# Squares of the keys in a prompt's attention summed from two rounded parts, one or two turns later

## The reference, cut to what matters

```python
def rmsnorm(x, g):
    xf = x.astype(jnp.float32)
    y = xf * lax.rsqrt(jnp.mean(xf * xf, axis=-1, keepdims=True) + EPS)
    return (y * g.astype(jnp.float32)).astype(x.dtype)

def mla_prompt(q_nope, q_rope, c_kv, k_rope, w_uk, w_uv, g_kn):
    k_nope = rmsnorm(jnp.einsum('btc,chd->bthd', c_kv, w_uk), g_kn)
    v = jnp.einsum('btc,chd->bthd', c_kv, w_uv)
    ...
        s = jnp.einsum('bqhd,bkhd->bhqk', qn, k_nope) + jnp.einsum('bqhr,bkr->bhqk', qr, k_rope)
        p = jax.nn.softmax(jnp.where(mask, s.astype(jnp.float32) * SOFTMAX_SCALE, -jnp.inf), axis=-1)
        return jnp.einsum('bhqk,bkhd->bqhd', p.astype(v.dtype), v)
```

## Time and the profile before

| | us |
|---|---|
| median of 3 runs | 1902.29 |
| lowest and highest | 1901.44, 1902.49 |
| the profiled execution | 1903.54 |
| its span in the trace | 1901.7 |
| TensorE busy in it | 1872.1 (98%) |
| VectorE, ScalarE, GpSimd busy | 1098.8, 904.0, 806.1 |

### The profile page before, as it was taken

The page is one execution under the profiler, slowest core; times in us unless marked ns, Lnnn a source line. Parts: engine busy times, 40 slices in busy tenths (PEclk is TensorE's granted clock), DMA queues, the critical chain, the costliest instruction groups (busy, mean ns, idle before and its releaser), DMA issues.

```text
span 1901.7 us, 35322 instructions
## 1 busy us (share of the span) xinstructions
PE 1872.1 (98%) x13021; PEld 1802.9 (95%) x13021; DVE 1098.8 (58%) x1950; ACT 904.0 (48%) x1858; POOL 806.1 (42%) x814
## 2 busy tenths in 40 slices
PE   7999999999999999999999999999999999999998
PEld 7886679999999999999999999999999999999998
DVE  4677756565556555544645644547773564564464
ACT  4456655554555455343424333347754342433333
POOL 3340013432223224253473474385755347347435
PEclk9999999999999999999999999999999999999999
DMA  5320101211111110222333232232222233323223
GB/s 153 67 57 3 26 20 44 80 33 47 35 39 32 48 35 17 71 80 78 89 89 88 78 98 81 79 109 78 75 79 78 78 88 90 88 83 95 77 86 97
DMA packets 253093, 131.63 MB, mean 69 GB/s; under 512 B 43073, under 2 KB 250754, under 8 KB 252882
## 3 DMA queue, kind: packets, MB, share of 16 engines
q1 hardware_dynamic: 252514, 128.56, 24.2%
q10 hardware_dynamic: 444, 1.29, 0.2%
HBM read 126.21 MB, written 3.61 MB: 68 GB/s over the span
## 4 chain that ended last, share of the span: by engine, by line
PE 94%; DVE 3%; ACT 1%; issue 1%; DMA 1%; SPq 0%; POOL 0%; DVEq 0%; ACTq 0%; POOLq 0%
PE ps L208 13%; PE ps L211 13%; PE ps L209 13%; PE ps L1275 7%; PE ps L1273 7%; PE ps L1274 7%; PE ps L1912 5%; PE ps L1910 5%; PE ps L1916 5%; PE ps L1303 3%; PE ps L259 2%; PE ps L251 2%; PE ps L252 2%; PE ps L1049 2%; PE ps L1240 2%; PE ps L265 1%
## 5 line engine op out<-in xcount | busy, mean ns | idle before, releaser
L208 PE MATMUL ps<-split,whi 128*128 128x288 f32 x1840 | 541.6, 296 | 1.4 <-DVE arena L807 1.0
L209 PE MATMUL ps<-split,whi 128*128 128x288 f32 x1840 | 539.0, 294 | 0.0
L211 PE MATMUL ps<-split,wlo 128*128 128x288 f32 x1840 | 526.7, 295 | 0.0
L195 POOL TENSOR_TENSOR wlo<-raw,whi 128x1024 fp32r<-128x1024 f32 x127 | 307.4, 2423 | 377.7 <-ACT whi L172 370.3
L208 PEld LDWEIGHTS ps<-split,whi 128*128 128x128 f32 x1840 | 345.3, 188 | 3.7 <-issue 3.0
L209 PEld LDWEIGHTS ps<-split,whi 128*128 128x128 f32 x1840 | 345.2, 188 | 0.4
L211 PEld LDWEIGHTS ps<-split,wlo 128*128 128x128 f32 x1840 | 339.9, 188 | 0.0
L1273 PE MATMUL ps<-split,split 128*128 128x384 f32 x768 | 268.2, 349 | 0.0
L1523 DVE TENSOR_REDUCE ssq<-arena 128x16 f32<-128x1024 f32 x128 | 156.1, 1220 | 186.6 <-ACT arena L1385 186.6
L1385 ACT ACTIVATE arena<-ps 128x384 f32<-128x384 f32 (+1 forms) x384 | 174.7, 457 | 184.4 <-PE ps L1275 181.4
L1275 PE MATMUL ps<-split,split 128*128 128x384 f32 x768 | 257.9, 336 | 0.0
(11 more groups left out here) (343 smaller groups left out, 3587.3 us busy)
## 6 DMA issues: line engine op xcount, KB each, us to landing
raw<-in_ffn_w_up SPq DMA_DIRECT2D x96, 512.0 KB, 3.7
raw<-in_ffn_w_down SPq DMA_DIRECT2D x48, 512.0 KB, 3.9
arena<-in_cache_ckv SPq DMA_DIRECT2D x128, 128.0 KB, 2.0
raw<-in_rec_w_in SPq DMA_DIRECT2D x16, 512.0 KB, 3.9
raw<-in_attn_w_o SPq DMA_DIRECT2D x8, 512.0 KB, 5.3
raw<-in_rec_w_out SPq DMA_DIRECT2D x8, 512.0 KB, 4.3
raw<-in_attn_w_down SPq DMA_DIRECT2D x7, 512.0 KB, 7.4
raw<-in_attn_w_uq SPq DMA_DIRECT2D x48, 64.0 KB, 2.1
```

What stands on the lines that cost most here:

```text
L195: pool.tensor_tensor(wlo[:, t % RING, :], raw[:, t % RING, :], f32(whi[:, t % RING, :]), ALU.subtract).then_inc(w_lo, 1)
L208: pe.matmul(o, wh, a, start=first, stop=False, skip_group_check=resumed)
L209: pe.matmul(o, wh, b, start=False, stop=False, skip_group_check=resumed)
L211: mm = pe.matmul(o, wl, a, start=False, stop=last, skip_group_check=resumed)
```

## The change

The sum of squares for pairs 1 to 7 is no longer a float32 product. ScalarE rounds the squares to float32r (`ksq_hi`), GpSimd subtracts that from the squares (`ksq_lo`, written over `sq[0]`), and TensorE multiplies both with a float32r copy of the ones (`blk64_hi`, made once on ScalarE), in four products. `key_sum` and `key_root` stand in unit 5 where they stood in unit 4, and `key_norm` in unit 6 where it stood in unit 4 (unit 5 for pair 1). The buffer `work` is allocated ahead of `smallg`.

```diff
+        k_hi, K_HI0 = u_ss, 12
+        k_lo, K_LO0 = u_rs, 12
+        ksq_hi = area(A_P + 7424, T, dt=F32R)
+        ksq_lo = nc.alloc_sbuf_tensor_at("ksq_lo", [P, T], F32R, offset=work_at)[:]
+        blk64_hi = area(A_P + 8000, P, dt=F32R)
+
         def key_sum(pe, j):
-            pe.wait_ge(k_sq, j + 1)
-            ones_product(pe, 4, blk64, sq[0]).then_inc(k_ss, 1)
+            if j == 0:
+                pe.wait_ge(k_sq, 1)
+                ones_product(pe, 4, blk64, sq[0]).then_inc(k_ss, 1)
+                return
+            pe.wait_ge(k_lo, K_LO0 + j)
+            for i, h, l in zip(range(2), halves(ksq_hi), halves(ksq_lo)):
+                pe.matmul(ps[:, 4 + i, 0:HT], blk64_hi, h, start=True, stop=False)
+                mm = pe.matmul(ps[:, 4 + i, 0:HT], blk64_hi, l, start=False, stop=True)
+            mm.then_inc(k_ss, 1)
+
+        def key_low(pool, j):
+            pool.wait_ge(k_hi, K_HI0 + j)
+            pool.tensor_tensor(ksq_lo, sq[0], f32(ksq_hi), ALU.subtract).then_inc(k_lo, 1)
+            pool.wait_ge(k_lo, K_LO0 + j)
...
         def key_square(act, j):
             act.wait_ge(k_ev, j + 1)
             act.activation(sq[0], kflat[j], ACT.Square).then_inc(k_sq, 1)
+            if j:
+                if j == 1:
+                    act.copy(blk64_hi, blk64)
+                act.wait_ge(k_sq, j + 1)
+                act.copy(ksq_hi, sq[0]).then_inc(k_hi, 1)
...
-                    if u % 8 == 4 and h // 2 < 7:
+                    if u % 8 == 5 and h // 2 < 7:
                         key_sum(pe, h // 2 + 1)
...
-                if u < UNITS and u % 8 == 4 and u // 8 < 7:
+                if u < UNITS and u % 8 == 5 and u // 8 < 7:
                     key_root(act, u // 8 + 1)
...
-                    if (u == 5 or u % 8 == 4 and u > 4) and h // 2 < 7:
+                    if u % 8 == 6 and h // 2 < 7:
                         key_norm(dve, h // 2 + 1)
...
+            for j in range(1, 8):
+                key_low(pool, j)
             sample_pool(pool)
```

More of the change, by code:

```diff
@@ L95, in build @@
         rpar = sb("rpar", [P, DC, R_ALL])
+        work_at = nc.sbuf_base
+        work = sb("work", [P, 5 * T])
         smallg = sb("smallg", [P, 12])
-        work = sb("work", [P, 5 * T])
         snew = sb("snew", [P, NB, HQ])
```

## The result

The changed kernel takes 1924.9 us, the median of 4 executions (1921.1 to 1931.4), against 1902.4 before: the ratio is 1.012, with a 95% interval from 1.0107 to 1.0133, some 22 us slower. The prediction had 1913.2 with a range up to 1917. Sign and place were right; the size forecast, 10.9 us, was half of what came. The profiled execution of one experiment, e11, was slow (2026.9 us at a mean clock of 0.851) and is left out of every ratio.

A forecast was written before the change was run, and what follows sets the result against it. TensorE was taken to bound the stage, closely, in a relay with VectorE and ScalarE. Five pairs (8.2 us), one (1.9) and pair 1 (0.8) gave 10.9 us, from 1902.3 to 1913.2 us, range 1907.5 to 1917.

The forecast's parts named there:

- The term that decides, root and placing without cover: Behind unit 5's scores: next head's scores wait for placed keys, starting 5.20 us later instead of 3.66; 1.54 us per covered pair.
- The hole where the sum stood: Behind unit 4's scores: the turn waits for ScalarE's copy behind the rounding; the 1.08 us saved is lost, 0.1 added.
- The sum of the waits: Over pairs 1 to 7: five at 1.64 us, one at 1.9, pair 1 at 0.8, together 10.9 us slower.
- The exponentials behind the copy slip by 0.7, but `attend` covers them: On ScalarE behind the turned row's copy: exponentials come 0.7 us later, hidden under the products of `attend`.
- GpSimd's subtraction: Between rounding and new sum: takes 1.43 us, has 2.3 us of slack, costs nothing.
- The rival that GpSimd and VectorE hold each other up: In pair 1, subtraction beside VectorE's scaling of unit 3's row: 0.5 to 1.5 us added, 1914 to 1915; 10 in 100.
- TensorE's saving as a gain of 3.8 us if nothing waited: Cheaper sum products on TensorE, 0.54 us a pair over seven pairs; as the faster rival 1898.5 us, 6 in 100.

The follow-up runs named there:

- e11: Kernel before with squares summed as float32r high part alone and, in the six covered pairs, the root ahead of unit 4's exponential: 1899.5 us (0.9982).
- e10: Changed kernel with an extra float32 product where the old sum stood, and the root of pairs 1 to 7 without its logarithm: 1916.8 us (1.0073).
- e1: Changed kernel with one unneeded float32 product of the old sum's shape where the old sum stood, in seven pairs: 1915.2 us (1.0065).
- e9: Changed kernel with an unneeded float32 product only ahead of each pair's first scores, the wait ahead of the turn left idle: 1923.9 us (1.011).
- e4: Changed kernel with ScalarE's rounding moved behind the copy of the turned row: 1913.3 us (1.0056).
- e7: Kernel before with only the rounding added on ScalarE behind the square, its result unused: 1908.1 us (1.0026).
- e8: Kernel before with squares of pairs 1 to 7 rounded and summed in float32r alone, low part left out, old places: 1902.6 us (0.9998).
- e2: Kernel before with only the move of sum, root and placing to units 5, 5 and 6, sum still float32: 1914.1 us (1.0058).
- e3: Changed kernel with sum, root and placing back in their old places: 1925.5 us (1.012).

## Why the prediction was wrong, point by point

- *The term that decides, root and placing without cover:* right. Keys 5.27 us behind unit 5's scores against 5.20; the wait of 1.03 us; the maximum of unit 7 at the placing's end (182.52 against the placing's 180.96 + 1.64). One sentence was too sharp: the chain is closed by ScalarE's root with only 0.15 us to spare against VectorE's own order (e10).
- *The hole where the sum stood:* right in place, short in size. "The turn can start at 198.27, that is 0.1 later than with the float32 sum": it is 0.28 later from the pair's first scores (190.22 - 182.75 = 7.47 against 198.17 - 190.98 = 7.19), since the square comes 0.08 later in its pair (5.47 us behind the first scores, 188.22 - 182.75, against 5.39, 196.37 - 190.98) and the turn follows the copy's end by 0.14 us, not by 0.04.
- *The sum of the waits:* 10.9 forecast, 12.6 measured with the clock held (e1). Five pairs at about 1.91 instead of 1.64, the pair with the extra work on VectorE 2.07 instead of 1.9, pair 1 1.01 instead of 0.8 (with the clock low behind its wait of 1.24 us it lost 2.06 in the changed kernel).
- *The step that failed* is that both waits were priced by their length alone. The prediction laid rows taken at full clock one behind the other ("at full granted clock") and never asked whether the clock would stay there with TensorE idle for 1.3 us in one piece. It did not: 1.7 us in each of six `attend`, 1.1 us in pair 1, and 9.7 us in the median of the changed kernel against that of e1. e1 shows the cause by taking only the idle away, e9 that in pairs 2 to 7 it is the wait ahead of the turn, e4 that with 0.7 us less of it `attend` runs at full clock. The Trainium skill, page "TensorE: Matmul & The Clock Gate", section "What's actually happening", says that the clock is set "based on how busy the PE has been recently" and knows the same two levels; the traces agree (0.57 over the 4.0 us behind the wait, 1.00 with it filled). The trace of the kernel before had a warning of its own, on none of the rows: TensorE stands idle for 3.57 us up to 18.15 us, and works at the lower level behind that.

```profile
14.60:18.10 3.50, 0.00 (x0) 0.00 (x0) 1.96 (x5) 2.90 (x5) 2.31 (x4) 0.91 1.05 359
18.10:24.20 6.10, 6.05 (x25) 5.85 (x26) 6.05 (x6) 4.57 (x7) 3.31 (x2) 0.50 0.51 99
```

A second case could have been priced from rows 2: the products of `attend` at half the clock, at most 2.37 us more in each of six pairs, so up to 14 us on top of 1913.2 (an estimate). 3.57 us is not 1.3, so the kernel before alone doesn't say whether the wait of the change is long enough.
- *"The exponentials behind the copy slip by 0.7, but `attend` covers them":* true in the changed kernel, where ScalarE is idle for 4 us there, and not as a rule: with the root still under `attend` the same slip costs 5 us (e7).
- *GpSimd's subtraction:* right, 1.40 us, in time in all pairs but the first. There a weight load of TensorE waits 0.45 us for it, and its products pause for 0.1 (the mask product ends at 159.75, the sum starts at 159.87). (What the prediction calls a product of GpSimd's in rows 7 is a subtraction too.) The rival that GpSimd and VectorE hold each other up shows in pair 1 alone, where the scaling of unit 3's row takes 0.92 instead of 0.49 us beside the subtraction:

```profile
158.41 1.40 POOL L1035 TENSOR_TENSOR ksq_lo<-work,split 128x576 fp32r<-128x576 f32 x1 [16.21 <-ACT split L1049]
...
159.18 0.92 DVE L1173 TENSOR_SCALAR work<-work,cols 128x512 f32<-128x512 f32 x1
```

- *TensorE's saving as a gain of 3.8 us if nothing waited:* too kind to the change. The chain through ScalarE and VectorE is as long as TensorE's own work in this stage (in e8 the pairs take 13.45 us as before), and a saving on TensorE alone gives nothing (e8) until the chain is shortened too (e11).

## What to carry to other kernels

A wait on TensorE is not priced by its length: look whether it leaves TensorE idle in one piece with a dense stretch of products behind it, and price those products at half the clock as a second case. What the clock did then is read from the windows of the trace and not from the row of a wait. Where the row view shows waits of an off-path engine under a long block of products, as here the root and the placing under `attend`, that block is their cover, and work moved out from under it must find new cover of the same length. An engine busy for 98% can still be only one of two bounds: a cheaper product gains only if the relay through the other engines has slack left.

## What the runs showed of the hardware that was not expected

- Idle of 1.3 us ahead of `attend` took its 16 products from 2.37 to some 4.0 us, in all six pairs of the changed kernel's trace and in four of the six in e9's; idle of 0.6 us at the same place did not in any pair of e4 or e2. Where between them it turns, and why e9's last two pairs differ, stays open.
- Two waits behind pair 7, about 1.0 (0.87 in e10) and 0.6 us with 0.7 us of products between them, brought the clock down in the traces of the changed kernel, e4 and e10 and left it at 1.00 in e1 and e2. The low stretch behind them lasted 3 to 4 us in e4 and e10 and 10 us in the changed kernel.
- The changed kernel scattered by 10 us from one execution to the next (1921 to 1931) and its time went with its mean clock, where the kernel before scatters by about 3; e9, with the same wait, scattered by 6, but e3, with a wait of 2.3 us, by 1.5 only.
- A float32 product of 576 columns, in two halves of 288, done for nothing in each of seven pairs (e1) made the kernel 10 us faster than it was without it.
